# U's high part made ahead of the gelu in the expert loop of a two-block layer stack

## The reference, cut to what matters

```python
def peer_ffn(h, w_q, sub_k1, sub_k2, expert_u, expert_v):
    ...
    def per_chunk(args):
        xc, ec, gc = args
        u = expert_u[ec]
        a = jnp.einsum('cd,chkd->chk', xc, u).astype(jnp.float32)
        w = (jax.nn.gelu(a) * gc).astype(xc.dtype)
        return jnp.einsum('chk,chkd->cd', w, expert_v[ec])
```

## Time and profile before

| | |
|---|---|
| time, median of 3 runs | 1788.64 us (1788.61 to 1788.73) |
| the profiled execution's own time | 1788.58 us |
| its span | 1786.8 us |
| PE busy | 1752.3 us, 98% of the span |
| DVE, ACT, POOL busy | 1345.2, 980.0, 500.1 us |
| granted TensorE clock | 0.999 of full speed |
| the loop changed here | about 514 to 1121 us of the span |

### The profile page before, as it was taken

One profiled execution on the slowest core, in us unless ns is written; L12 is line 12 of the kernel. 1 busy time (PEld: TensorE's weight loads), 2 busy tenths in 40 slices (PEclk: granted clock), 3 DMA queues, 4 the chain that ended last, 5 costly groups with the idle time before them and its releaser, 6 DMA issues.

```text
span 1786.8 us, 30696 instructions
## 1 busy us (share of the span) xinstructions
PE 1752.3 (98%) x10764; PEld 1546.5 (87%) x10764; DVE 1345.2 (75%) x2466; ACT 980.0 (55%) x1679; POOL 500.1 (28%) x245
## 2 busy tenths in 40 slices
PE   8998999999999999999999999999999999999998
PEld 7995899899888888888888888877999988989997
DVE  6757849899767777777777777876579965669974
ACT  5567555479444444444444444666565545556553
POOL 0150166379144444444444444000000000000000
PEclk9999999999999999999999999999999999999999
DMA  7660454601555555555556665644455564535562
GB/s 293 203 232 13 155 189 153 224 25 48 169 185 188 188 190 190 191 191 192 189 193 226 232 223 188 242 142 165 143 193 188 188 196 149 177 129 178 189 196 75
DMA packets 84719, 313.70 MB, mean 176 GB/s; under 512 B 9360, under 2 KB 9488, under 8 KB 83216
## 3 DMA queue, kind: packets, MB, share of 16 engines
q1 hardware_dynamic: 82912, 304.44, 50.4%
q10 hardware_dynamic: 1712, 7.97, 1.3%
HBM read 304.77 MB, written 7.60 MB: 175 GB/s over the span
## 4 chain that ended last, share of the span: by engine, by line
PE 52%; issue 25%; ACT 9%; DVE 7%; DMA 3%; POOL 1%; PEld 1%; ACTq 1%; DVEq 0%; SPq 0%; POOLq 0%; PEldq 0%
PE bank L798 47%; ACT wsplit L1757 6%; PE bank L1249 3%; DMA raw<-expert_u 3%; DVE act_e L2353 2%; DVE wsplit L2347 2%; POOL wsplit L1400 1%; ACT projq L1579 1%; ACT probs L1579 0%; PEld bank L1249 0%; PE bank L843 0%; PE bank L832 0%; DVE wsplit L1891 0%; DVE projq L2106 0%; DVE att L2092 0%
## 5 line engine op out<-in xcount | busy, mean ns | idle before, releaser
L798 PE MATMUL bank<-HT,wsplit 128*128 128x256 f32 (+1 forms) x5056 | 720.0, 301 | 1.3 <-DVE HT L1934 0.9
L798 PEld LDWEIGHTS bank<-HT,wsplit 128*128 128x128 f32 x5056 | 679.3, 189 | 46.5 <-issue 2.6
L1431 POOL TENSOR_TENSOR wsplit<-raw,wsplit 128x1024 fp32r<-128x1024 f32 x111 | 289.6, 2609 | 370.6 <-ACT wsplit L1757 370.6
L2347 DVE TENSOR_TENSOR wsplit<-raw,wsplit 128x1024 fp32r<-128x1024 f32 x127 | 326.3, 2569 | 64.4 <-ACT wsplit L1757 64.3
L798 PE MATMUL bank<-wsplit,wexp 128*128 128x512 f32 x1536 | 373.4, 393 | 0.7 <-DVE wexp L2372 0.6
L798 PEld LDWEIGHTS bank<-wsplit,wexp 128*128 128x128 f32 x1536 | 279.4, 188 | 58.2 <-DVE wsplit L2347 1.9
L1757 ACT ACTIVATE wsplit<-raw 128x1024 fp32r<-128x1024 f32 x238 | 238.3, 1046 | 30.0 <-PE bank L798 26.8
L1765 ACT ACTIVATE act_e<-act_e 128x256 f32<-128x256 f32 x112 | 46.8, 418 | 317.6 <-DVE act_e L2353 317.6
L1466 ACT ACTIVATE wsplit<-raw 128x1024 fp32r<-128x1024 f32 x148 | 156.4, 1059 | 111.5 <-PE bank L798 110.5
L1891 DVE TENSOR_TENSOR wsplit<-raw,wsplit 128x1024 fp32r<-128x1024 f32 x124 | 154.5, 1258 | 78.5 <-ACT wsplit L1466 77.7
L1891 DVE TENSOR_TENSOR wsplit<-raw1b,wsplit 128x1024 fp32r<-128x1024 f32 x102 | 122.6, 1221 | 43.9 <-ACT wsplit L1466 43.5
(11 more groups left out here) (288 smaller groups left out, 2032.9 us busy)
## 6 DMA issues: line engine op xcount, KB each, us to landing
raw<-weights SPq DMA_DIRECT2D x148, 512.0 KB, 4.2
raw<-expert_v SPq DMA_DIRECT2D x127, 512.0 KB, 3.7
raw<-expert_u SPq DMA_DIRECT2D x119, 512.0 KB, 4.4
raw1b<-weights SPq DMA_DIRECT2D x102, 512.0 KB, 4.3
raw1a<-weights SPq DMA_DIRECT2D x48, 512.0 KB, 4.7
early_u<-expert_u SPq DMA_DIRECT2D x5, 512.0 KB, 3.6
raw1a<-expert_u SPq DMA_DIRECT2D x4, 512.0 KB, 3.8
parked<-memT SPq DMA_DIRECT2D x1, 2048.0 KB, 7.3
```

The costliest lines, as they stand in the source:

```text
L798: ins = pe.matmul(out, lhsT, rhs, start=start, stop=stop, **kw)
L1431: pool.tensor_tensor(wsplit[:, s, 1, :], raw0[:, s, :], f32(wsplit[:, s, 0, :]), ALU.subtract).then_inc(u_lo, 1)
L2347: dve.tensor_tensor(wsplit[:, 2 + s, 1, :], src, f32(wsplit[:, 2 + s, 0, :]), ALU.subtract).then_inc(v_lo, 1)
```

## The change

In the body of the loop, and in the two experts written out ahead of it, the function `gelu` is cut in two. The copy of the low half stays in front, and U's high part of `e+2` now comes between that copy and the gelu of `e`. V's high part still comes last. Nothing else changes.

```diff
-            def gelu(e, s):
+            def low_half(e, s):
 
                 act.wait_ge(a_full, e + (1 - EARLY))
                 act.wait_ge(a_w, e + (BEGIN - 1))
                 act.activation(act_e[:, s, :], PS[s][:, S:2 * S], ACT.Copy).then_inc(a_lo, 1)
+
+            def gelu(e, s):
+
                 act.wait_ge(a_sum, e + (1 - EARLY))
                 act.activation(act_e[:, s, :], act_e[:, s, :], ACT.Gelu_apprx_tanh).then_inc(a_gelu, 1)
...
             def block_parts(i, s):
 
-                gelu(i * 2 + s, s)
+                low_half(i * 2 + s, s)
                 if isinstance(i, int) and s == 0:
                     first_part(u_landed[1], 16, a_mul, EARLY, u_hi, 1, raw0[:, 1, :])
                 first_part(u_landed[s], i * 16 + (32 - 8 * EARLY), a_full, i * 2 + (s + 1 - EARLY), u_hi, s, raw0[:, s, :])
+                gelu(i * 2 + s, s)
                 first_part(v_landed[1 - s], i * 16 + (16 if s == 0 else 32) - 8 * V_RING, a_v, i * 2 + (s + BEGIN), v_hi, 3 - s,
                            raw0[:, 3 - s, :])
...
+            low_half(NKEYS - 2, 0)
             gelu(NKEYS - 2, 0)
             first_part(v_landed[1], 8 * (NKEYS - V_RING), a_v, NKEYS - 2 + BEGIN, v_hi, 3, raw0[:, 3, :])
             limit[0] = len(UNITS)
             split_to(FIRST2 + 1)
+            low_half(NKEYS - 1, 1)
             gelu(NKEYS - 1, 1)
```

## The result

The changed kernel takes 1814.91 us (median, 1814.23 to 1816.44) against 1788.62 of before in the same session: the ratio is 1.0149, 95% interval 1.0136 to 1.0161. It is slower by 26 us, and the forecast was 1811. The profiled execution has a span of 1813.4 us, 26.6 more than before.

What follows compares the result with a forecast made beforehand. PE (about 5.5 us per expert), tied with an ACT-POOL-DVE circle, was taken as the bound. Terms +11.7 outside the ten extra-transfer pairs, +11.8 inside and -1 gave +22.5 on 1788.6: 1811 us, range 1793 to 1829.

Steps and rivals of the forecast that it cites:

- Two circles tied, hardly 3 us to be had: Loop before: PE's work, about 5.5 us per expert, and an ACT-POOL-DVE circle of 5.49 us; at most 3 us to gain.
- POOL is always first, and the product waits to 0.28 after its end: Changed loop: POOL's low part of U starts 0.37 us before DVE's gate multiply, which ends 0.28 us after POOL.
- `wexp` fits by 0.14 us: Changed loop: expert weights ready 5.18 us after times_v starts, against 5.36 allowed by PE's need; stated slack 0.14 us.
- The circle over two experts by U's landing, 11.31 us: Loop: late U landing delays POOL, multiply, V's low part and next U issue; 11.31 us per two experts against 11.05.
- The ten pairs, +11.8: Ten pairs of loop steps with extra transfers: U lands after 5.6 us, 12.36 us per pair against 11.18; +11.8 us.
- A first pair or two run in, -1: Start of the loop: a first pair or two pass before the circle over two experts closes, taking off 1 us.
- M + 4.1: Kernel before: U's issue time, counted from M, the start of PE's times_v; 5.2 us were there for landing.
- no landing of U under 4.0: Loop transfers of U: the trace shows none landing in under 4.0 us, against the skill's estimate of 3.2 us.

Runs made afterwards that it cites:

- experiment 4: The changed kernel with the gelu's output and the product with the gates in two PSUM banks instead of SBUF: 1791.26 us, ratio 1.0012.
- experiment 3: The changed kernel with SyncE's transfers shifted by one, U of e+1 issued ahead of V of e: 1797.27 us, ratio 1.0048.
- Experiments 1: The changed kernel with the old order (copy, gelu, U's high part) in the two experts written out ahead of ScalarE's loop: 1807.16 us, ratio 1.0104.
- experiment 2: The kernel before, with the new order only in the two experts written out ahead of ScalarE's loop: 1796.91 us, ratio 1.0044.

## Why the prediction was right, point by point

- *Two circles tied, hardly 3 us to be had.* Right. Every version that opens the circle needs 604.0 to 605.9 us for the 110 steps against 607.1, and the best is 2.7 us faster than before (1786.24 against 1788.89).
- *POOL is always first, and the product waits to 0.28 after its end.* Right: 0.29 in the timeline, and experiment 4 took it away by changing where the operation reads and writes. Only the step at 528.57, right behind the entry, has the product ahead of POOL; there the cast behind it was held instead, for 2.38 us. The Trainium skill's rule on the shared ports ("SBUF — State Buffer", section "Who interferes with whom") says that the order of issue decides who blocks, and that a DVE operation with at most one input in SBUF doesn't contend, unless it runs in a mode that uses two ports, as casts can. By that rule, both the 2.23 us of L2374 and its 0.43 us in experiment 4 agree, and so does the cast L2376, which has one input in SBUF and was held at the entry. Which mode it ran in, no run here shows.
- *`wexp` fits by 0.14 us.* Right. With U early the loop runs at 5.51 us with the product held on (experiment 3).
- *The circle over two experts by U's landing, 11.31 us.* The mechanism was right: the experts shown take 11.36, with a landing of 4.70. As a mean it was a little large: 2 x 5.61 = 11.22 from 600 to 900 us. Some landings are quick enough for a pair to go at PE's pace, and V's low part starts 0.08 us before the end of the subtraction. Outside the ten pairs the term was +11.7, and 17.7 - 10.7 = 7.0 were measured. The prediction counted all 45 pairs outside the ten alike, but the last ones, behind the ten, lose nothing. There U is issued 0.38 us behind V instead of 0.87. By the prediction's own sum the circle is then some 10.8 us, under PE's 11.0 (2 x 5.51). No run changes this interval alone, so this reason is argued and not shown.
- *The ten pairs, +11.8.* Right: +10.7 us were measured. The prediction had 12.36 us for a pair, and 122.5 / 10 = 12.25 were measured.
- *A first pair or two run in, -1.* This term had the wrong sign and the wrong size: the entry cost 8.9 us. The prediction followed the loop's steady body and let the two written-out experts ahead of it pass. There the moved gelu stands behind two landings of U, not one, and POOL works on two low parts while the gelu's product waits. Experiments 1 and 2 put this cost at 8.1 us (26.3 - 18.2) and 7.9 us (1796.9 - 1789.0).
- *Two slips that changed nothing in the sum.* The prediction says that a U was issued at M + 4.1 "of the expert two before"; its 5.2 us fit only the expert just before (5.50 + 3.85 - 4.1 = 5.25). And "no landing of U under 4.0" holds for the earlier trace rows alone: over all 78 transfers of L740 in the kernel before the shortest landing is 3.5 us.

So the mechanism of the loop was right, and that the forecast of +22.5 came as near as it did to +26 is in part luck: the two terms of the loop were 5.8 us too large together, the entry was 9.9 us too small, and the two errors partly cancel.

## What to carry to other kernels

When an instruction is moved ahead of another on an in-order engine, the moved one gives up its own wait, and the one it passed takes over that of the moved one: here the gelu took over the wait for U's transfer. Follow what the earlier result sets off on the other engines; POOL's earlier start moved its hold on DVE from V's low part to the product, which PE waits for sooner, and the transfers, issued behind that DVE work, closed a circle over two experts. And work through the code ahead of the loop by itself, since its waits are not those of the steady state.

## What the runs showed of the hardware that was not expected

After PE had stood for 5.76 us, its next 12 matmuls ran at a granted clock of 0.50 (1.2 GHz) for 5.3 us; in experiment 2 the same happened. After the 3.52 us that PE stood at the entry in experiment 4, the mean granted clock of the next 4.4 us was 0.62 (first row below). After the 2.16 us that PE waited for the next `wexp` of the changed kernel, up to 526.37, the clock was 1.00 (second row). Waits of PE in the loop, of up to 1.3 us, left it at 1.00 in every window of 20 us from 950 to 1050.

```profile
510.40:514.80 4.40, 4.38 (x13) 3.48 (x14) 2.67 (x1) 0.00 (x0) 1.59 (x1) 0.62 0.50 146
...
526.40:529.20 2.80, 2.80 (x12) 2.33 (x13) 2.08 (x4) 0.42 (x1) 2.80 (x7) 1.00 0.17 37
```

The rounding of 256 float32 columns to fp32r, with one input in SBUF, was held by POOL like the product: 2.31 us instead of 0.29 at the entry. With its input in PSUM it took 0.42 us beside POOL.

A U of 512 KB that was issued 2.2 us ahead of V landed after 3.7 us in the median (3.4 to 4.3, experiment 3), and after 4.4 (4.0 to 4.9) when it was issued 0.6 to 0.9 us behind V.
